# Two branches' scores, transposes and values placed a quarter of a weight chunk later in a hybrid decoder's mixer

## The reference

```python
def mixer_block(x, ...):
    xn = rms_norm(x, norm_g)
    proj = xn @ w_in                       # 1024 x 8200: q, k, v of three branches, gates
    y_sb = merge_heads(stick_breaking_attention(q, k, v))            # branch 0, 8 heads x 64
    y_mb = merge_heads(moba_attention(q, k, v))                      # branch 1, 8 heads x 64
    y_ml = merge_heads(mlstm_chunkwise(q, k, v, log_i, log_f)) * jax.nn.sigmoid(ml_o)  # branch 2, 4 heads x 128
    y = jnp.einsum("nbsw,nwd->nbsd", branches, w_branch)             # 3 x (512 x 1024)
    gates = jax.nn.sigmoid(gate_logits.reshape(bsz, s, N_BRANCH, D_MODEL))
    merged = jnp.einsum("bsnd,nbsd->bsd", gates, y)
    return x + merged @ w_out

def reference(x, ...):
    for l in range(DEPTH):                 # DEPTH = 2
        x = mixer_block(x, ...)
        x = hier_moe_block(x, ...)         # top 1 of 4 groups, then top 2 of 8 experts in it
    return x
```

## Time and profile before

| what | us |
|---|---|
| median of 3 runs | 1022.61 (1022.32 to 1024.69) |
| the profiled execution | 1026.03 |
| its span | 1024.1 |
| TensorE busy in the span | 974.4 (95%) |
| VectorE busy | 480.4 (47%) |
| ScalarE busy | 466.0 (46%) |
| share of the DMA queue of all weights | 74.7% |

### The profile page before, as it was taken

One profiled execution on the slowest core, in us unless ns is written; L12 is line 12 of the kernel. 1 busy time (PEld: TensorE's weight loads), 2 busy tenths in 40 slices (PEclk: granted clock), 3 DMA queues, 4 the chain that ended last, 5 costly groups with the idle time before them and its releaser, 6 DMA issues.

```text
span 1024.1 us, 19187 instructions
## 1 busy us (share of the span) xinstructions
PE 974.4 (95%) x8030; PEld 789.2 (77%) x8030; DVE 480.4 (47%) x845; ACT 466.0 (46%) x719; POOL 23.7 (2%) x42
## 2 busy tenths in 40 slices
PE   8999999999999999977999999999999999999777
PEld 8898899899986666633598988998998866666444
DVE  6446775577853132211183567655587632222112
ACT  6456655566543433311275454565655443343111
POOL 1010100000000000000000100000000000000000
PEclk9999999999999999978899999999999999999889
DMA  9634545546888999999975245545659799999996
GB/s 311 228 125 164 171 164 165 207 168 244 300 359 329 401 420 420 419 420 421 391 241 201 83 164 172 198 133 206 243 209 353 305 360 418 419 420 420 420 420 247
DMA packets 85510, 293.36 MB, mean 286 GB/s; under 512 B 17008, under 2 KB 17072, under 8 KB 60848
## 3 DMA queue, kind: packets, MB, share of 16 engines
q1 hardware_dynamic: 85424, 292.12, 74.7%
HBM read 291.05 MB, written 1.05 MB: 285 GB/s over the span
## 4 chain that ended last, share of the span: by engine, by line
PE 82%; DMA 9%; DVE 4%; ACT 3%; issue 1%; SPq 1%; ACTq 0%; DVEq 0%
PE ps_a L781 10%; PE ps_a L783 10%; PE ps_a L782 10%; PE ps_b L1105 9%; DMA units_over_branches<-in_w_dram 5%; PE ps_b L1125 5%; PE ps_b L1184 5%; PE ps_a L1168 5%; PE ps_a L765 5%; PE ps_a L767 4%; PE ps_a L766 4%; DMA units_over_splits<-in_w_dram 3%; PE ps_b L1054 2%; PE ps_b L992 1%; PE ps_b L884 1%
## 5 line engine op out<-in xcount | busy, mean ns | idle before, releaser
L1216 ACT ACTIVATE w_high<-weight_ring 128x1024 fp32r<-128x1024 f32 x166 | 174.9, 1059 | 203.9 <-PE ps_a L783 145.0
L1502 DVE TENSOR_TENSOR w_low<-weight_ring,w_high 128x1024 fp32r<-128x1024 f32 x168 | 202.9, 1225 | 126.6 <-ACT w_high L1216 124.2
L781 PE MATMUL ps_a<-xnT_high,w_high 128*128 128x256 f32 x704 | 201.5, 286 | 2.3 <-DVE xnT_low L1508 2.3
L783 PE MATMUL ps_a<-xnT_high,w_low 128*128 128x256 f32 x704 | 199.5, 283 | 0.0
L782 PE MATMUL ps_a<-xnT_low,w_high 128*128 128x256 f32 x704 | 198.9, 282 | 0.0
L781 PEld LDWEIGHTS ps_a<-xnT_high,w_high 128*128 128x128 f32 x704 | 133.5, 190 | 4.5 <-issue 4.5
L782 PEld LDWEIGHTS ps_a<-xnT_low,w_high 128*128 128x128 f32 x704 | 133.6, 190 | 0.5 <-issue 0.5
L783 PEld LDWEIGHTS ps_a<-xnT_high,w_low 128*128 128x128 f32 x704 | 132.9, 189 | 0.0
L1881 DVE TENSOR_TENSOR y_lo<-ps_b,y_hi 128x512 fp32r<-128x512 f32 x64 | 44.3, 692 | 146.1 <-ACT y_hi L1467 144.0
L1184 PEld LDWEIGHTS ps_b<-fold,h 128*128 128x128 f32 x512 | 70.6, 204 | 34.2 <-issue 29.2
L1428 ACT ACTIVATE h<-ps_b 128x512 f32<-128x512 f32 x64 | 38.3, 598 | 126.8 <-PE ps_b L1105 126.8
(11 more groups left out here) (337 smaller groups left out, 1580.0 us busy)
## 6 DMA issues: line engine op xcount, KB each, us to landing
weight_ring<-in_w_in_dram SPq DMA_DIRECT2D x62, 1024.0 KB, 5.2
units_over_splits<-in_w_dram SPq DMA_DIRECT2D x60, 1024.0 KB, 23.1
units_over_attention<-in_w_dram SPq DMA_DIRECT2D x46, 1024.0 KB, 16.3
weight_ring<-in_w_dram SPq DMA_DIRECT2D x40, 1024.0 KB, 20.7
units_over_branches<-in_w_dram SPq DMA_DIRECT2D x30, 1024.0 KB, 18.4
weight_ring<-in_w_branch_dram SPq DMA_DIRECT2D x12, 1024.0 KB, 5.2
unit_over_gates<-in_w_dram SPq DMA_DIRECT2D x10, 1024.0 KB, 17.9
weight_ring<-in_w_out_dram SPq DMA_DIRECT2D x8, 1024.0 KB, 5.8
```

The lines of the kernel that those rows point to most:

```text
L781: mm(dst, wh, xh, start=row == 0 and s % 2 == 0, stop=False, skip_group_check=True)
L783: last = mm(dst, wl, xh, start=False, stop=row == rows - 1, skip_group_check=True)
L1216: A(mix_buf(whi, i), mix_raw(i), ACT.Copy).then_inc(hi_ready, 1)
L1502: v.tensor_tensor(mix_buf(wlo, i), mix_raw(i), mix_buf(whi, i).bitcast(F32), ALU.subtract).then_inc(lo_ready, 1)
```

## The change

The same instructions are issued on every engine. Only TensorE's order changes, in both layers. `project` and `branch` can now do some quarters of a chunk, so that a small step can stand between two quarters. The second branch's second scores move from ahead of g4 to behind its first quarter; its second transposes from ahead of g5 to behind its first quarter; the third branch's transposes from behind the first branch's projection to behind the second branch's first quarter; and the third branch's values from behind the second quarter of the second branch to behind the third.

```diff
-        def project(name):
+        def project(name, parts=range(PARTS)):
...
-            for q in range(PARTS):
+            for q in parts:
...
-        def branch(b, halves=(0, 1)):
+        half_pair = [None]
+
+        def branch(b, quarters=range(PARTS)):
             pe.wait_ge(*((sb_e, 2), (mb_e, 2), (ml_e, 1))[b])
-            for half in halves:
-                pair = take_pair()
-                for q in range(2):
-                    by_feature(PARTS * (FIRST_BRANCH + b) + 2 * half + q, pair, [x[:, b] for x in brT], q, NC)
+            for n in quarters:
+                if n % 2 == 0:
+                    half_pair[0] = take_pair()
+                by_feature(PARTS * (FIRST_BRANCH + b) + n, half_pair[0], [x[:, b] for x in brT], n % 2, NC)
...
         mb_scores(0); project("g2"); probs_T(mb_p, 1, mb_pt); project("g3"); mb_out(0)
-        mb_scores(1); project("g4"); probs_T(mb_p, 2, mb_pt); project("g5"); mb_out(1)
-        branch(0, [0]); ml_scores(); branch(0, [1]); probs_T(ml_p, 1, ml_pt); branch(1, [0]); ml_out()
-        branch(1, [1]); branch(2)
+        project("g4", [0]); mb_scores(1); project("g4", [1, 2, 3]); project("g5", [0]); probs_T(mb_p, 2, mb_pt)
+        project("g5", [1, 2, 3]); mb_out(1)
+        branch(0, [0, 1]); ml_scores(); branch(0, [2, 3]); branch(1, [0]); probs_T(ml_p, 1, ml_pt)
+        branch(1, [1, 2]); ml_out(); branch(1, [3]); branch(2)
```

## The result

The changed kernel takes 1016.21 us (median of 4 runs, 1016.16 to 1016.52) beside 1022.97 us of the kernel before (4 runs, 1022.32 to 1024.69): 6.8 us less, ratio 0.993 (95% interval 0.9916 to 0.9944). Two later measurements, each with six runs of it and 23 of the kernel before, gave ratios of 0.994 (0.9920 to 0.9959) and 0.994 (0.9922 to 0.9957), which is 6.1 us; their medians differ by 6.3 and 5.4 us. The forecast was 1018.4 us, a gain of 4.2 us, and its range began at 1016.3.

What follows compares the result with a forecast made beforehand. The mixer was taken as bound by TensorE, the experts by their weights' transfers. Terms of -1.8, -1.52, +0.3, +1.0, -0.15 and +0.1 gave -2.1 us a layer, -4.2 in all: 1022.61 to 1018.4 us, range 1016.3 to 1021.4 (8 in 10).

Steps and rivals of the forecast that it cites:

- part 5: Output projection behind the branches: TensorE's 0.2 us lateness behind VectorE's differences goes; -0.15 us a layer, bounds 0 and -0.3.
- parts 3 and 4: Third branch's transposes moved: wait goes, -1.52 us a layer; new waits for merge, +0.3, and third branch's input, +1.0 us.
- Parts 1 and 2: Second branch's second scores and transposes a quarter later: 1.92 us wait goes, none at the transposes; net -1.8 us a layer.
- The clock: Rule that removed waits also give back clock: granted clock beside the first wait 1.00, so nothing added.
- Does the gain reach the end: Experts' stage: starts from buffers that TensorE frees and moves forward with it, so the 4.2 us gain counts whole.
- R3: Transfers hold the end, giving the gain back before the experts' first step: 1022.6 us, or 1020.5 with half; chance 0.12.
- R4: Experts' last stretch: a second batch of half-speed work falls behind the last long transfer; 3.8 us slower, 1026.4 us; chance 0.06.
- R1: Third branch's new wait, 2.2 us, with 0.6 us at the merge, eats its gain: 1021.0 us; chance 0.14.
- R2: Third branch's new waits at nothing to 0.3 us: gain 3.1 us a layer, 1016.4 us; chance 0.08.

Runs made afterwards that it cites:

- values_back: The changed kernel with the third branch's values again behind the second branch's second quarter, not the third; ratios 0.994 and 0.9919 to the kernel before.
- pad22: The changed kernel with 22 idle matmuls of 128 columns between the first and second chunk in each layer; ratio 1.0065 to the kernel before.

## Why the prediction was wrong

The sign, the places and the mechanism were right; the size wasn't, 4.2 us against 6.1 to 6.8. The mixers account for 5.56 us, 1.4 us more than the sum: part 5 gave 0.9 us of that, parts 3 and 4 gave 0.55 us. What lies between 5.56 and 6.8 is in no step of the mixers; the clock's falls and spread can make it up. By its own steps:

**Parts 1 and 2: right.** Forecast -1.8 us a layer, measured -1.79 and -1.77. The scores start at 200.32 and the transposes at 213.55, with no wait.

**Parts 3 and 4: right in each wait, 0.3 us off in the sum.** The wait for the merge is 0.28 us (the third quarter starts at 246.67, the matmul before it at 246.27, where 0.12 is usual), forecast 0.3; it is too short for the list of waits, where I had expected it. The wait at the third branch's projection is 0.79 us by the list and 0.94 and 0.96 us by the distance of the matmuls in the two layers, forecast 1.0. From the second low part to the start of the third branch's projection it came to -0.40 us in both layers, forecast -0.12. The term mis-sized is the removed wait: I took the list's 1.52 us although my own rows had 244.90 - 243.22 = 1.68 us, and counted restarts on top.

**Part 5: the failed step.** I took 0.15 us a layer for VectorE's late differences at the output projection and bounded it at 0.3, from one matmul of the first layer. Measured, from the start of the third branch's projection to the addition, are 0.45 and 0.75 us. TensorE was late at both halves of the output projection: in the first layer 272.11 against 271.91 at the first and 0.17 us at the second, and slower by some 0.1 us in the matmuls behind each wait; and the second layer, which I had called the first one moved by 506.65 us, has a first start of this kind, with the last matmul ahead of it:

```profile
778.43 0.28 PE L783 MATMUL ps_a<-branchT_parts,w_low 128*128 128x256 f32 x1
...
779.03 0.47 PE L765 MATMUL ps_a<-w_high,xnT_high 128*128 128x512 f32 x1 [0.31 <-issue]
```

That is 0.48 us late. The list names no releaser, but VectorE's difference (L1695) ends at 778.93, 0.1 us before. I never looked at the second layer there. Counted from the first low part, the start of the third branch's projection is 2.2 us earlier in the changed kernel and VectorE's first difference for the output projection 2.8 us, so all of the lateness goes: 267.71 follows 267.60 without a gap. VectorE gains the more because ScalarE's second split behind its copy for the third branch (L1345, L1348 after) had to wait until TensorE had used a quarter, and no longer has to. ScalarE before and after:

```profile
260.65 1.06 ACT L1216 ACTIVATE w_high<-weight_ring 128x1024 fp32r<-128x1024 f32 x1 [1.44 <-PE ps_a L783]
...
254.69 1.99 ACT L1219 ACTIVATE w_high<-weight_ring 128x1024 fp32r<-128x1024 f32 x2
```

VectorE's low part of that quarter waited 1.09 us for it (before, at 261.75) and doesn't wait now. In values_back, where the values stand a quarter earlier again, ScalarE's split waits 0.31 us.

**The clock: a rule weighed against one execution.** The Trainium skill, TensorE: Matmul & The Clock Gate, A second HAM failure mode, tells of a kernel in which frequent short idle times between groups of matmuls make the clock fall and rise. I set it aside because the granted clock beside the wait was 1.00. In 3 of 12 layers it did fall behind this wait, at 1.51 to 1.58 us each. By the estimate above this adds 0.8 us to the mean gain: 5.56 + 0.8 = 6.4 us, between the 6.1 and 6.8 measured; spread of the experts' stages alone could do the same. The trace of the forecast could not decide on the rule: the fall is a thing that happens in some executions, and it was one sample.

**Does the gain reach the end: right.** R3 and R4 are out by the result itself, since at least the mixers' 5.56 us came out at the end; pad22 shows the same for a shift to later. On R4's reason: the half-speed stretches of the experts move about from run to run in every kernel, and their stages vary by 3.7 and 3.2 us over all kernels. My distance of 3.4 us between the first trace and the median was such spread too, with the lower clock at its start in it.

**R1 and R2.** R1's long wait didn't come: the two new waits are 0.28 and 0.94 to 0.96 us, not 0.6 and 2.2. R2's time, 1016.4 us, is within 0.2 us of the measured 1016.21, but that is luck: in R2 the new waits hardly appear, and they did appear, at the size of the forecast.

**The range.** It took in R2 (1016.4) by its gain, but no case in which several small terms err to the same side, and none in which the clock adds to the gain.

## What to carry to other kernels

A wait of an engine that sets the end was worth the distance between the instructions around it here (1.68 us, where the list had 1.52), and the short waits further down the same chain go with it when the chain that causes them speeds up: look at each of them in each layer before doubling. Moving the instruction that waits also moves the start of what it feeds; move the consumer too, or the wait comes back there. TensorE's clock can be lower behind a wait near 2 us in some executions and not in others, so one trace at full clock doesn't clear the wait: look at the same place in several. And split the difference of two traces by stage first, since 4.3 of the 9.9 us between the first two here lay outside the stretch that the change touches.

## What the runs showed of the hardware

- Behind a wait of 1.9 us TensorE's clock fell to its lower level (1.2 GHz) in 2 of 10 layers, and behind one of 2.3 us in 1 of 2, for some 3.4 us, and work at 0.12 us a matmul ran at 0.215. Behind the third branch's wait of 1.7 us it did in none of the 20 layers that have that wait unfilled.
- A matmul of 128 columns with both operands in plain f32 was recorded as two and took 0.22 to 0.25 us, a transpose of 128 columns 0.11 us.
- In the experts' stages, bound by transfers, the length varied between 194.6 and 198.9 us. From the first low part to the addition of the output projection the same kernel repeated to 0.03 us unless the clock fell; the way from the start of the span to the first low part varied by 2.5 us, more than 1 us of which goes with the clock there.
